# RWKV recurrence with the scores one turn ahead, and the modulation sums moved to other places

## What is computed

```python
c_act = jax.nn.silu(c)
for i in range(DEPTH):
    mod = c_act @ ada_w[i] + ada_b[i]
    sh1, sc1, g1, sh2, sc2, g2 = [t[:, None, :] for t in jnp.split(mod, 6, axis=-1)]
    h = _rms(x) * (1.0 + sc1) + sh1
    y = _rwkv7_mix(h, ...)          # i == 0; the mLSTM mixer for i == 1
    x = x + g1 * y
    h = _rms(x) * (1.0 + sc2) + sh2
    x = x + g2 * _swiglu(h, ffn_w_gu[i], ffn_w_down[i])

def _rwkv7_step(state, inp):        # over 512 tokens, 16 heads of 64
    r_t, w_t, k_t, v_t, a_t, b_t = inp
    sa = jnp.einsum('bhvk,bhk->bhv', state, a_t)
    state = state * w_t[:, :, None, :] + sa[..., None] * b_t[:, :, None, :] + v_t[..., None] * k_t[:, :, None, :]
    y = jnp.einsum('bhvk,bhk->bhv', state, r_t)
    return state, y
```

## Time and profile before

| what | value |
|---|---|
| median of 3 runs | 2796.61 us (2796.05 to 2798.64) |
| profiled execution, own time | 2793.61 us |
| its span, first to last instruction | 2791.7 us |
| mean granted clock of TensorE | 0.962 |
| busy shares: TensorE, VectorE, ScalarE, GpSimd | 92%, 43%, 35%, 34% |
| stage of the recurrence | 239 to 503 us |
| output stage, products from 565.9 | 503 to 616 us |
| first feed-forward, second half from 872 | 616 to 998 us |

### The profile page before, as it was taken

The page is one execution under the profiler, slowest core; times in us unless marked ns, Lnnn a source line. Parts: engine busy times, 40 slices in busy tenths (PEclk is TensorE's granted clock), DMA queues, the critical chain, the costliest instruction groups (busy, mean ns, idle before and its releaser), DMA issues.

```text
span 2791.7 us, 33786 instructions
## 1 busy us (share of the span) xinstructions
PE 2578.8 (92%) x14024; PEld 2007.7 (72%) x14024; DVE 1194.2 (43%) x1794; ACT 981.7 (35%) x1446; POOL 955.0 (34%) x334
## 2 busy tenths in 40 slices
PE   7996676779999988998999999989899999999999
PEld 5755665368887867876887878868687777777686
DVE  5465875854343353344111343434306424343604
ACT  4652443323322233443332333222324334433523
POOL 2312121433444433443444433413433333222232
PEclk8997988889999999999999999999999999999999
DMA  6113443024555421112222332202122222111121
GB/s 259 65 71 104 129 110 86 31 76 158 194 189 194 152 91 69 53 66 80 96 90 104 136 126 94 102 31 91 39 105 77 94 79 103 61 46 54 45 92 61
DMA packets 93396, 272.10 MB, mean 97 GB/s; under 512 B 54864, under 2 KB 54992, under 8 KB 65488
## 3 DMA queue, kind: packets, MB, share of 16 engines
q1 hardware_dynamic: 91248, 265.52, 27.1%
q10 hardware_dynamic: 2016, 4.72, 0.5%
HBM read 264.44 MB, written 5.78 MB: 97 GB/s over the span
## 4 chain that ended last, share of the span: by engine, by line
PE 77%; DVE 11%; ACT 4%; DMA 3%; issue 3%; POOL 2%; SPq 1%; ACTq 0%; DVEq 0%; POOLq 0%
PE bank L342 20%; PE bank L344 19%; PE bank L343 19%; PE bank L278 2%; PE bank L276 2%; PE bank L277 2%; PE bank L2614 1%; PE bank L3139 1%; DMA inverse<-scratch_inverse 1%; POOL ring_low L373 1%; ACT w_high L363 1%; DVE conv_out L2340 1%; PE bank L2860 1%; PE bank L3127 1%; DVE probs L3336 1%
## 5 line engine op out<-in xcount | busy, mean ns | idle before, releaser
L373 POOL TENSOR_TENSOR ring_low<-ring,w_high 128x2048 fp32r<-128x2048 f32 (+2 forms) x184 | 800.8, 4354 | 1348.4 <-ACT w_high L363 1348.4
L342 PE MATMUL bank<-h_high,w_high 128*128 128x512 f32 (+1 forms) x1304 | 523.3, 401 | 28.3 <-DVE h_low L453 20.0
L344 PE MATMUL bank<-h_high,ring_low 128*128 128x512 f32 (+1 forms) x1304 | 520.2, 399 | 0.0
L343 PE MATMUL bank<-h_low,w_high 128*128 128x512 f32 (+1 forms) x1304 | 517.5, 397 | 0.0
L363 ACT ACTIVATE w_high<-ring 128x2048 fp32r<-128x2048 f32 (+2 forms) x184 | 330.9, 1801 | 389.2 <-PE bank L344 373.1
L342 PEld LDWEIGHTS bank<-h_high,w_high 128*128 128x128 f32 (+1 forms) x1304 | 247.1, 189 | 94.5 <-issue 27.4
L343 PEld LDWEIGHTS bank<-h_low,w_high 128*128 128x128 f32 (+1 forms) x1304 | 246.9, 189 | 60.6 <-issue 0.7
L344 PEld LDWEIGHTS bank<-h_high,ring_low 128*128 128x128 f32 (+1 forms) x1304 | 246.6, 189 | 60.3
L342 PE MATMUL bank<-z_high,w_high 128*128 128x512 f32 x384 | 154.3, 402 | 12.5 <-DVEq L1859 6.4
L344 PE MATMUL bank<-z_high,ring_low 128*128 128x512 f32 x384 | 153.8, 400 | 0.0
L343 PE MATMUL bank<-z_low,w_high 128*128 128x512 f32 x384 | 152.8, 398 | 0.0
(11 more groups left out here) (440 smaller groups left out, 4479.6 us busy)
## 6 DMA issues: line engine op xcount, KB each, us to landing
ring<-in_stream SPq DMA_DIRECT2D x210, 1024.0 KB, 4.8
ada_slot<-in_ada_next SPq DMA_DIRECT2D x48, 512.0 KB, 3.2
scale_weights<-in_first SPq DMA_DIRECT2D x4, 1024.0 KB, 19.1
inverse<-scratch_inverse SPq DMA_DIRECT2D x16, 256.0 KB, 4.4
w_first<-in_first SPq DMA_DIRECT2D x2, 1024.0 KB, 7.6
x_res<-in_x SPq DMA_DIRECT2D x2, 1024.0 KB, 12.0
scratch_rows<-scores SPq DMA_DIRECT2D x16, 128.0 KB, 2.6
x_res<-in_x ACTq DMA_DIRECT2D x1, 2048.0 KB, 8.3
```

Of the source, the lines that this page charges most:

```text
L342: pe.matmul(out, w_high[:, k, cols], x_high, start=start, stop=False)
L343: pe.matmul(out, w_high[:, k, cols], x_low, start=False, stop=False)
L344: return pe.matmul(out, w_low[:, k, cols], x_high, start=False, stop=stop)
L373: pool.tensor_tensor(self.c.ring_low[:, b % SLOTS, 0:cols], self.c.ring[:, b % SLOTS, 0:cols], self.high_buf[:, b % 2, 0:cols].bitcast(F32 ...
```

## The change

The loop over the turns of `rwkv_chunks` now runs from -1 to KD+1 and has three pairs in work. In turn p: the scores, masks and transposes of pair n = p+1, the solve of pair p, the steps from the inverse for pair q = p-1, and `results` (outer products, copies, results) for pair o = p-2. The scores go to banks 4 to 7. `SC` and `UV` get a third buffer, `XY` and `Lm` a second, and these lie in slots 1 to 3 of the weight ring, which is otherwise not used in this stage. GpSimd's levels wait for the first product of p-2 and not of p-1. SyncE's `turn(p+1)` (scores out, blocks in) stands behind the read of the inverse of p.

Half of the modulation rows leave the stage: one block (two tiles, `next_ada(p)`) a turn is left, behind the masks, loaded into slot 0 by SyncE. The rows of g1 (8 tiles) go to `rwkv_output`, between the last `finish` and the first residual; the rows of g2 (8 tiles, of either layer) go to that layer's `ffn`, between the last gate-up tile and the first residual. Both are loaded by two DMAs of 2 MB each on ScalarE's queue. In `ffn(0)` 40 tiles remain instead of 48.

```diff
@@ rwkv_chunks
+    ada_slot = chip.over("ada_slot", [P, SLOT], F32, chip.ring_offset)
+    spare = chip.ring_offset + 4 * SLOT
+    SC.append(chip.over("scores_2", [P, 2, NC_, 3 * CHUNK], F32, spare))
+    UV.append(chip.over("u_v_2", [P, NC_, 2, CHUNK], F32, spare + 24 * NC_ * CHUNK))
-    XY = chip.keep("inverse_16", [P, 2, NS, CHUNK])
+    XY = [chip.keep("inverse_16", ...), chip.over("inverse_16", ..., spare + 32 * NC_ * CHUNK)]
+    Lm = [Lm0, chip.over("level", [P, NS, CHUNK], F32, spare + 40 * NC_ * CHUNK)]
-    b_ada = chip.take_blocks(ADA_LAYER - ADA_FIRST)
@@ tensor
+        def first_product(q):
+            inv_in.wait(pe, q)
+            level.wait(pe, q, 1)
+            if q + 1 < KD:
+                a_out.wait(pe, q + 1)
+                v_out.wait(pe, q + 1)
+            both(4, 5, ...Lm[q % 2]..., t1_mm)
+        def results(q):
+            y2_out.wait(pe, q)
+            t1_out.wait(pe, min(q + 1, KD - 1))
+            r_out.wait(pe, min(q + 2, KD - 1))
+            t2_out.wait(pe, q)
+            outer(q, 0)
+            outer(q, 1)
...
-        for p in range(KD + 1):
-            q = p - 1
-            A, B = p < KD, p >= 1
+        for p in range(-1, KD + 2):
+            n, q, o = p + 1, p - 1, p - 2
+            A, B, C = n < KD, 0 <= q < KD, 0 <= o
+            if B:
+                first_product(q)
+            if C:
+                results(o)
+            if A:
+                keyed.wait(pe, n)
...
+                scores(n, 0)
+                scores(n, 1)
+                masked.wait(pe, n)
+                keys(n)
+                rows_and_values(n)
             if B:
                 t1_out.wait(pe, q)
+                if C:
+                    n_out.wait(pe, o)
+                    o_out.wait(pe, o)
+                    g_out.wait(pe, o)
+                    r_add.wait(pe, o)
                 both(0, 1, ..., x1_mm)
                 both(2, 3, ..., y1_mm)
...
@@ vector
+        for p in range(-1, KD + 2):
+            if solves:
+                solve_blocks(p)
+            if C:
+                y1_out.wait(dve, o)
+                merge(o, y2_mm, y2_out, Y1, Y1, 2)
+            if solves:
+                solve_corner(p)
             if A:
+                key(n)
+                mask(n)
+            if C:
+                for par in range(2):
+                    g_out.wait(dve, o, par)
+                    ...r_add
+            if solves:
+                next_ada(p)
             if B:
+                merge(q, x1_mm, x1_out, X1, X[:, 0, :, :], 0)
+                merge(q, y1_mm, y1_out, Y1, X[:, 1, :, :], 2)
@@ gpsimd
-            if p:
-                t1_mm.wait(pool, p - 1)
+            if p >= 2:
+                t1_mm.wait(pool, p - 2)
@@ sync
-        for n in range(SLOTS):
-            chip.load(sp, b_ada + n)
+            if p:
+                ada_sum.wait(sp, p - 1)
+            sp.dma_start(ada_slot[:, :], chip.io["first"][6 + p]).then_inc(ada_in.sem, 16)
+        turn(0)
+        for p in range(KD):
+            ...inverse of p out and in
+            if p + 1 < KD:
+                turn(p + 1)
+        ada_sum.wait(sp, KD - 1)
+        gr_mm.wait(sp, KD - 3)
+        no_mm.wait(sp, KD - 3)
+        y1_out.wait(sp, KD - 1)
@@ rwkv_output, scalar
         act.dma_start(chip.x[:, :, :], ...).then_inc(x_back.sem, 16)
+        for n in range(2):
+            act.dma_start(g1[n][:, :, :], chip.io["gains"][0, 0, n]).then_inc(g1_in[n].sem, 16)
@@ rwkv_output, vector, before residual
+        for n in range(KD):
+            dve.wait_ge(g1_in[n // 4].sem, g1_in[n // 4].landed)
+            ada_tile(chip, dve, g1[n // 4][:, n % 4, :], 2 * KD + n).then_inc(g1_sum.sem, 1)
@@ ffn, scalar
         by_four(act, KF, gate)
+        act.wait_ge(chip.gemm_done, 2 * (b0 + KF))
+        for n in range(2):
+            act.dma_start(gain_w[:, 4 * n:4 * n + 4, :], chip.io["gains"][layer, 1, n]).then_inc(gain_in[n].sem, 16)
@@ ffn, vector
+        for n in range(KD):
+            dve.wait_ge(gain_in[n // 4].sem, gain_in[n // 4].landed)
+            ada_tile(chip, dve, gain_w[:, n, :], m + 40 + n).then_inc(gain_sum.sem, 1)
```

More of the change, by code:

```diff
@@ L647, in vector @@
         pass
-ADA_FIRST, ADA_LAYER = 8, 24
 def ada_tile(chip, dve, weights, col):
@@ L1451, in scalar @@
+            if n + 1 < KD:
+                grow(n + 1)
+            if A:
+                if n >= 3:
+                    gr_mm.wait(act, n - 3)
+                for i in range(2):
+                    bk_mm.wait(act, n, i)
+                    act.activation(SC[n % 3][:, :, 4 * i:4 * i + 4, 0:CHUNK].rearrange("p h c n -> p c h n"),
+                                   chip.bank[6 + i][:, :].rearrange("p (c h n) -> p c h n", h=2, n=CHUNK), ACT.Copy)\
                        .then_inc(bk_out.sem, 1)
-                av_mm.wait(act, p, 0)
@@ L1459, in scalar @@
+                if n >= 3:
+                    no_mm.wait(act, n - 3)
+                V, v_ = UV[n % 3], chip.bank[5][:, :].rearrange("p (c h n) -> p c h n", h=2, n=CHUNK)
                 act.activation(V[0:64, 1:NC_:2, :, :], v_[0:64, :, :, :], ACT.Copy).then_inc(v_out.sem, 1)
@@ new lines, in vector @@
+        for p in range(-1, KD + 2):
+            n, q, o = p + 1, p - 1, p - 2
+            A, B, C = n < KD, 0 <= q < KD, 0 <= o
+            solves = 0 <= p < KD
+            if solves:
+                solve_blocks(p)
+            if C:
+                y1_out.wait(dve, o)
+                merge(o, y2_mm, y2_out, Y1, Y1, 2)
+            if solves:
+                solve_corner(p)
+            if A:
+                key(n)
+                mask(n)
+            if C:
+                for par in range(2):
+                    g_out.wait(dve, o, par)
+                    r = systems(f.r, o)[:, par:NC_:2, :]
+                    dve.tensor_tensor(r, bank(2 + par, P)[:, :, CHUNK:P], r, ALU.add).then_inc(r_add.sem, 1)
+            if solves:
+                next_ada(p)
@@ L1605, in vector @@
-            if A:
-                solve_corner(p)
-            if p + 1 < KD:
-                key(p + 1)
-            if A:
-                next_ada(2 * p + 1)
-            if B:
-                for par in range(2):
-                    g_out.wait(dve, q, par)
-                    r = systems(f.r, q)[:, par:NC_:2, :]
-                    dve.tensor_tensor(r, bank(2 + par, P)[:, :, CHUNK:P], r, ALU.add).then_inc(r_add.sem, 1)
+                merge(q, y1_mm, y1_out, Y1, X[:, 1, :, :], 2)
         def decay_of(g, c):
@@ L3593, in ada_tiles, with gain_tiles @@
     return np.ascontiguousarray(i["ada_w"][layer].T.reshape(48, P, D))
+def gain_tiles(i):
+    return np.stack([ada_tiles(i, layer).reshape(2, 3, 2, KD // 2, P, D)[:, 2].transpose(0, 1, 3, 2, 4)
+                     for layer in range(2)])
 def ada_blocks(i, first, last):
```

302 lines of the change are left out of this document (128 added, 174 removed).

## The result

| | before | after |
|---|---|---|
| median | 2796.33 us (2795.45 to 2798.64, 4 runs) | 2778.8 us (2777.63 to 2781.51, 4 runs) |
| profiled execution, its span | 2791.7 us | 2775.8 us |
| mean granted clock of TensorE | 0.962 | 0.968 |

The ratio is 0.9937, with a 95% interval of 0.992 to 0.9955: faster, by 17.5 us between the medians and 15.9 between the spans. The forecast was 2782.7, a gain of 13.9 us.

The account below looks back on a forecast made before the run. The eight turns were taken as bound by a loop of waits with a DRAM trip in each. The terms -25.3 - 1 + 9.4 + 0.9 + 2.1 = -13.9 gave 2782.7 us, range 2767 to 2797.

Parts of the forecast that it names:

- Start: Before the first store of solved blocks: four weight loads and two tiles go, -1 us, bounds 0 and -1.8.
- Seven intervals: Between the eight stores of solved blocks: 20.7 + 6 x 22.9 = 158.1 us against 183.4, -25.3.
- Without the lock the turn would be near 21.4: In a steady turn: if VectorE's tiles and GpSimd's levels did not block each other, tiles end at 18.1, turn near 21.4.
- SyncE's path 21.6: In a steady turn: masks, row store and row read land by 21.6 us, under VectorE's 22.7.
- Rival 2: In the turns: tiles slip past GpSimd and the clock stays up, turns of 21.4, total 2768 us; chance 0.10.
- Tail: From the eighth solve to the last r_add: results of pair 6 join the chain, +9.4 us, bounds +7 and +14.
- Output stage: In the output stage: two more DMA issues precede ScalarE's first rounding, +0.9 us; the later first residual costs nothing.
- Feed-forwards: In both second halves: the gain rows delay ScalarE's fourth rounding, 0.4 and 1.7, together +2.1 us, bounds 0 and +10.
- rival 3: In the feed-forwards: the 4 MB of loads land late; at 35 us, +22.9 in all, 2819 us; chance 0.08.
- Rival 1: In the turns and their end: TensorE partly stays at half clock, turns of 24.2, total 2795 us; chance 0.17.

Follow-up runs that it names:

- the doubled run: The changed kernel with each of the two ada tiles of a turn computed twice; 2815.84 us, ratio 1.0067.
- the run without tiles: The changed kernel without the two ada tiles of each turn and their 1 MB loads; 2781.95 us, ratio 0.9945.
- a tile before the masks: The changed kernel with one of a turn's two ada tiles moved between the keys and the masks; 2784.42 us, ratio 0.9964.
- the moves and the old turns: The kernel before with only the modulation rows moved, two tiles a turn; one load slot 2831.71 us, two slots 2799.74 us.
- the rows first: The changed kernel with SyncE issuing the next pair's row store and read ahead of the inverse's read; 2787.64 us, ratio 0.9965.
- one inverse buffer: The changed kernel with SyncE's row store and read ahead of the inverse's read, and single inverse and level buffers; 2816.82 us, ratio 1.007.

## Why the prediction was right, and where its sizes were off

The sum of -13.9 stands against -15.9 in the spans. The terms below add up to -13.2; the rest lies in stages that the change does not touch. That the sum came so near is in part luck: the seven intervals gained 3.4 less than forecast, and the tail cost 2.65 less. By its own terms:

- **Start**, -1: measured -1.35, from 26.06 to 24.71 between the stage's first instruction and the first store's issue.
- **Seven intervals**, -25.3: measured -21.9, the term most off. Of the 3.4, 0.9 lies in the base (182.5 by the issues, 183.4 by the chain of waits that I used). The first interval was 21.5 and not 20.7: the first operation of the block solve took 1.06 beside GpSimd's levels where it takes 0.15 alone, and in the runs without that meeting the interval was 20.6 to 20.9. The second was 24.2 and not 22.9: its scores ran at half clock behind 11.10 us of idle TensorE:

```profile
287.07 3.78 PE L1247 MATMUL bank<-rw_all,keys 64*128 64x128 f32 x32 [11.10 <-DVE keys L1522]
```

  I had written that the new order has no idle stretches of 2 us and more; in the second turn, where no results of an earlier pair fill TensorE's program, it has. The other five sum to 114.9 against 114.5 forecast. Their mechanism is the forecast one: VectorE from solve to merge, tiles and levels one by one. The rows of the changed kernel show the alternation, so does the doubled run, where four tiles take 1.91, 2.28, 2.27 and 2.27. This is the rule of the Trainium skill (SBUF — State Buffer, SBUF: two separate sides) that the prediction weighed; the trace agrees by the 2.29.
- **"Without the lock the turn would be near 21.4", SyncE's path 21.6**: shown, as far as turns at full clock go: 21.5 in the run without tiles and in the one with a tile before the masks. It is TensorE's path that sets them. In the turn of the run without tiles that starts at 330.49, VectorE waits 1.63 for the scores and 2.80 for the step products (340.45), and not for the rows, whose read was issued at 340.49 and takes 2.6, so that they land 0.2 ahead of the block solve at 343.33. What the prediction lacked is that this floor is not a stable one. VectorE's 22.7 hid rows that land up to 1.7 us late; take that cover away, and VectorE waits, the last merge is late, TensorE idles over 2 us, and the outer products and results run at 1.2 GHz. Rival 2 had the tiles and the clock as two independent pieces of luck, and they are bound together.
- **Tail**, +9.4: measured +6.75, under the lower bound of +7. The part behind outer(7) is as before (8.9 against 9.1). From the eighth store to outer(7) it is 29.45 against 22.5, +6.9. Of before it takes one line that the earlier trace rows do not have:

```profile
459.45 1.98 PE L1333 MATMUL bank<-step_t,inverse 64*64 64x64 f32 x32 [1.29 <-ACT step_t L1442]
```

  and of the changed kernel

```profile
434.83 1.10 PE L1299 MATMUL bank<-inverse,level 64*64 64x64 f32 x32
...
437.27 1.96 PE L1286 MATMUL bank<-rw_all,inv_t 64*64 64x128 f32 x32 [1.34 <-DVE inv_t L1576]
...
445.35 1.15 PE L1364 MATMUL bank<-step_t,inverse 64*64 64x64 f32 x32 [1.37 <-DVE rw_all L1609]
...
453.19 3.44 PE L1286 MATMUL bank<-rw_all,inv_t 64*64 64x128 f32 x32 [1.57 <-DVE inv_t L1576]
```

  The first product comes 11.09 behind the store instead of 9.77: +1.3, within the forecast's 1 to 2, of which the sum took the upper end. From outer(6) to the step products, which is `results(6)` with its copies and r_add, it is 8.08: the forecast's 6.7 + 1.3. But from the first product to the step products it was 3.26 before, with 1.29 of waiting for ScalarE's copy, and is 10.52 now: +7.3 and not +8, as `results(6)` covers that wait. And from the step products to outer(7) it is 7.84 instead of 9.50: -1.7, since the steps run at full clock (1.15 instead of 1.98), where the forecast gave back 0.6. So the path was the forecast one, and three of its steps had the wrong size: +1.3 for +2, +7.3 for +8 and -1.7 for -0.6.
- **Output stage**, +0.9: measured +1.08 from ScalarE's first DMA issue to the next stage's first product. The number is right by luck: the later square left TensorE idle for 2.27 us instead of 1.07 ahead of its second group of products, the next five groups took 1.9 to 2.1 instead of 1.0 to 1.1, and the products with the output weights began 2.3 later; 1.2 of it came back up to the next stage. The later first residual cost nothing, as forecast.
- **Feed-forwards**, +2.1 (0.4 and 1.7): measured 0.80 and 1.36 by the stage lengths, and 1.15 and 1.7 come back with the square behind the rounding, which shows the mechanism: VectorE's residual(0) behind the gains, ScalarE's square behind it, the rounding behind the square. In the second this is clear (398.6 to 399.8 us from reciprocal to `rho` in all runs with the moved rows and the old order of the square, 396.9 and 397.0 with the new one, 397.2 before). For the first the same three are 382.2 to 383.2, twice 381.9, and 382.2, so its 0.80 is no more than its spread. The loads were through in 17.0, near the 16.6 of the forecast, so rival 3 is out by 7 us. From there to the end of the first residual it was 8.0 and not 5.8, as one tile took 3.52 beside GpSimd's subtraction for `ring_low`, a meeting that the forecast left out.
- The stages that the change does not touch differ by -3.2 between the two profiled executions (-1.7 in the mLSTM stage, -1.5 behind the copy of `rho`), and +0.5 ahead of the stage. That is not explained. The other runs with these same stages were 0.7 to 3.6 us longer behind the copy of `rho`, so the changed kernel's profiled execution was a fortunate one there, and the 2 us by which the total was missed are smaller than it.

Rival 1 (half clock through the turns, 2795) did not come, but its mechanism did, in part: the clock sets the second interval and outer(7) (3.44 instead of 1.96), and in the runs without tiles and with a tile before the masks it took back what they should have gained. The tiles look like ballast in the turn; leaving them out gains nothing, and some 6 us (0.9917 against 0.9937, with overlapping intervals) only once TensorE is kept at work.

## What to carry to other kernels

When a wait is taken out of a loop of waits, look at which path is next and how steady it is: here a DMA round trip that varies by 2 us lay 1 us under the new bound, and each late one was charged twice, once as a wait and once as a TensorE that fell to half speed behind it. So read the idle time ahead of TensorE's groups together with their mean duration, in a good and a bad turn of the same run, before making another engine faster. Where short gaps couldn't be closed, a few products that nobody reads, about as long as the gap, held the clock here (six, 1.60 us, in gaps of 1.34 to 1.69); longer than the gap (eight, 2.05 us) they cost part of their excess in each turn.

## What had not been expected of the hardware

- The row store (two DMAs of 128 KB to DRAM, then the read) took 3.1 to 3.6 us from issue to the read's issue in all turns of the kernel before and in the first five of the reordered ones, but mostly 4.3 to 5.4 (3.2 to 3.7 at times) in their last three, also where no read of the inverse was in flight (4.41 to 4.66) and where no tile was loaded (4.42 to 4.95). It is not the new order alone: with the moves and the old turns it took up to 4.32 (one slot) and 3.99 (two). The store of the inverse (four DMAs) does the same, in the kernel before too: 3.3 us to the read's issue in its first four turns, 3.9 to 4.25 in the last four. The cause is open; no run separates it.
- Six 128x128 fp32 identity products take 1.60 us at full clock, 12 records, eight 2.05 us, 16 records: two records each.
- TensorE's level inside a turn: behind idle stretches of 2.4 to 4.5 us the outer products took 2.9 to 3.7 us, once (2.37) still 1.96. Behind 1.8 and less they took 1.96 in the turns of the kernel before and of the changed kernel. But behind 1.34 they took 3.33 to 3.68 in some turns with the rows first and in all with one inverse buffer, where the first product had itself waited for the inverse. And in the tail outer(7) took 3.38 to 3.68 behind 1.56 and 1.57 in the changed kernel and in the runs without fillers (3.61 in the kernel before), with several waits of 1.4 us and less ahead of it, but 1.96 behind 1.56 in the run with the moves and one slot. One gap's length alone does not tell it.
